# Input projection of the long-convolution block: seven products of half-size blocks in place of eight

## What is computed

```
def _centred_conv3(u, w, b):
    up = jnp.pad(u, ((0, 0), (1, 1), (0, 0)))
    return up[:, :-2] * w[0] + up[:, 1:-1] * w[1] + up[:, 2:] * w[2] + b

def _hyena_filters(L, ...):
    ...
    h = (a @ f_w3.astype(F32)).reshape(L, 2, HY_ORDER, D_MODEL)
    ...
    h = h * window[:, None, None, :]
    ...
    two_sided = two_sided / jnp.sum(jnp.abs(two_sided), 0, keepdims=True)
    return jnp.fft.rfft(two_sided, axis=0)

def _hyena(h, w_in, b_in, conv_w, conv_b, ...):
    u = _centred_conv3(h @ w_in + b_in, conv_w, conv_b)
    v, x1, x2 = jnp.split(u, 3, -1)
    ...
```

## Time and profile before

| | us |
|---|---|
| median of 3 runs | 3907.69 (3905.93 to 3911.46) |
| the profiled execution, its own time | 3907.51 |
| its span, first to last instruction | 3905.7 |
| PE busy in the span | 3610.5 (92%) |
| the stage's first matmul | at 58.87 |
| its last DVE copy to `u_staged` | from 496.05 to 496.74 |
| the next stage's first matmul | at 502.35 |

### The profile page before, as it was taken

The page is one execution under the profiler, slowest core; times in us unless marked ns, Lnnn a source line. Parts: engine busy times, 40 slices in busy tenths (PEclk is TensorE's granted clock), DMA queues, the critical chain, the costliest instruction groups (busy, mean ns, idle before and its releaser), DMA issues. The chain is left out here.

```text
span 3905.7 us, 63530 instructions
## 1 busy us (share of the span) xinstructions
PE 3610.5 (92%) x26142; PEld 2233.3 (57%) x26142; DVE 2554.0 (65%) x3451; ACT 884.7 (23%) x1758; POOL 461.4 (12%) x499
## 2 busy tenths in 40 slices
PE   6999989998879999999999998999976998868996
PEld 3444478884455555555555555544455898435563
DVE  5656379995876666767666674454076778557773
ACT  2000022221122221222212112322135443113232
POOL 0000000003100000000000001000031876001110
PEclk9999999998989999999999999999987999989998
DMA  7573322216589999999999995211002100228996
GB/s 278 218 261 138 143 76 109 117 76 239 219 285 361 335 328 327 326 335 329 328 328 333 332 325 205 89 56 70 33 1 90 37 4 4 100 92 315 357 357 226
DMA packets 289975, 798.58 MB, mean 204 GB/s; under 512 B 18728, under 2 KB 25904, under 8 KB 275120
## 3 DMA queue, kind: packets, MB, share of 16 engines
q1 hardware_dynamic: 271856, 719.02, 50.5%
q0 software_dynamic: 17136, 73.54, 5.9%
q10 hardware_dynamic: 720, 2.17, 0.2%
HBM read 708.56 MB, written 86.11 MB: 203 GB/s over the span
## 5 line engine op out<-in xcount | busy, mean ns | idle before, releaser
L1550 PE MATMUL banks<-moe_down,moe_hidT 128*128 128x512 f32 x1280 | 565.7, 595 | 9.4 <-DMA moe_down<-d_wd 9.3
L1550 PEld LDWEIGHTS banks<-moe_down,moe_hidT 128*128 128x128 f32 x1280 | 237.6, 191 | 281.5 <-issue 276.1
L1920 PE MATMUL banks<-hT,w_in_ring 128*128 128x512 f32 (+3 forms) x976 | 363.9, 535 | 1.9 <-ACT hT L1981 1.0
L518 PE MATMUL banks<-hT,w_in_ring 128*128 128x512 f32 x768 | 339.3, 596 | 1.4 <-PEq L212 1.4
L1623 ACT COPY moe_parts<-banks 128x512 f32<-128x512 f32 (+1 forms) x240 | 123.4, 514 | 840.7 <-PE banks L1529 837.7
L1529 PE MATMUL banks<-moe_wsums,moe_xsums 128*64 128x256 f32 x2560 | 301.3, 389 | 8.1 <-DVE moe_xsums L1667 4.0
L1920 PEld LDWEIGHTS banks<-hT,w_in_ring 128*128 128x128 f32 (+1 forms) x976 | 183.2, 188 | 180.7 <-issue 170.2
L1529 PEld LDWEIGHTS banks<-moe_wsums,moe_xsums 128*64 128x64 f32 x2560 | 181.1, 139 | 134.5 <-issue 49.1
L518 PEld LDWEIGHTS banks<-hT,w_in_ring 128*128 128x128 f32 x768 | 142.8, 190 | 185.2 <-issue 175.7
L757 PE MATMUL banks<-x_block,dft 128*128 128x256 f32 x896 | 196.5, 382 | 6.3 <-PEq L392 6.3
L757 PEld LDWEIGHTS banks<-x_block,dft 128*128 128x128 f32 x896 | 171.6, 192 | 30.3 <-issue 6.7
(11 more groups left out here) (479 smaller groups left out, 6015.8 us busy)
## 6 DMA issues: line engine op xcount, KB each, us to landing
moe_down<-d_wd SPq DMA_DIRECT2D x160, 1024.0 KB, 11.1
x_block<-d_wg SPq DMA_DIRECT2D x96, 1024.0 KB, 7.9
x_block<-d_wu SPq DMA_DIRECT2D x96, 1024.0 KB, 10.9
mix<-d_wg SPq DMA_DIRECT2D x64, 1024.0 KB, 8.8
mix<-d_wu SPq DMA_DIRECT2D x64, 1024.0 KB, 11.3
x_block<-d_seq SPq DMA_DIRECT2D x19, 1024.0 KB, 4.8
w_in_ring<-d_w_in SPq DMA_DIRECT2D x9, 2048.0 KB, 10.1
x_block<-d_mod_w SPq DMA_DIRECT2D x8, 2048.0 KB, 11.9
```

Source lines behind the costliest of these rows:

```text
L518: last = nc.tensor.matmul(m.ps[:, g % 2, :], ring[:, c, k, (mt % 4) * P:(mt % 4 + 1) * P], hT[:, k, h * BANK:(h + 1) * BANK], start=(k == ...
L1550: last = nc.tensor.matmul(m.ps[:, Y_BANK + h, :], hidT[:, j % 2, i * P:(i + 1) * P], wd[:, i, h * BANK:(h + 1) * BANK], start=(fc == 0 and ...
L1920: last = nc.tensor.matmul(m.ps[0:width, g % 6, 0:n], ring[:, q % 2, k, at:at + width], hT[:, k, first:first + n], start=(k == 0), stop=(k ...
```

## The change

Weights and tokens of the projection are cut into 2 by 2 blocks: two units make a pair (12 pairs, `n`), with `a11`, `a12` and `a21`, `a22` the lower and upper half of the channel sum for the first and second unit of the pair; `b11` to `b22` are the four quarters of `hT`. Each pair takes seven products P1 to P7 (Winograd's form of Strassen's scheme), each of 4 matmuls into one of banks 0, 1 and 5, in the order P1, P2, P6, P7, P5, P3, P4:

- The token sums `t1` to `t4` are made once, by DVE, as the stage starts (`t2` and `t4` lie in `x_block`, `t1` over `b12`).
- The weight sums are made by POOL, four sums of 128 by 512 in each pair, two of them in place in the ring.
- ACT writes only P1 (with the bias) to `u_padded`. DVE adds the other products from their banks (`added`), six times in a pair, and P7 in one sum of three operands: product, difference of the biases, and what was kept.
- `turn` is cut into single transposes of four tiles with one bank, 4, between them, spread over the next pair; `collect` likewise. `magnitudes` is cut in two.
- The window has one buffer: SP loads the next as soon as DVE has read the last. The matvec slots are halved (24 of 1 MB), since `t2` and `t4` take their room. In a pair SP loads slots 4n + 4 and 4n + 5, then stores `taps` of round n - 1 and loads the filter weights of round n + 1, then the window of round n + 1.
- At the end, `d_taps` of the next stage is loaded only after the last product.

```diff
@@ -180,8 +180,12 @@
...
-    sp.dma_start(m.window[:, b], m.dram["window"][j % NQ]).then_inc((m.ahead.win0, m.ahead.win1)[b], 16)
...
+def load_window(sp, m, j):
+
+    sp.dma_start(m.window[:], m.dram["window"][j % NQ]).then_inc(m.ahead.win, 16)
...
@@ -376,12 +381,11 @@
 
 def hyena_in_stage(nc, m):
...
+        nc.sbuf_tensor("token_diff", [P, KT // 2, BANK], F32) as t3,
+        nc.sbuf_tensor("w_diff", [P, KT // 2, P], F32) as s3,
...
         @block.sync
         def _(sp):
             def load_mv(n):
-                sp.dma_start(mv_ring[:, n % 2], mod_weights(m, GROUPS_IN[n // MV_SLOTS], n % MV_SLOTS)).then_inc(mv_in[n % 2], 16)
+                group, k = GROUPS_IN[n // KT], n % KT
+                name, at = ("mod_w", group) if group < MOD_GROUPS else ("ada_w", group - MOD_GROUPS)
+                sp.dma_start(mv_ring[:, n % 2], m.dram[name][:, k, at * MV_COLS:(at + 1) * MV_COLS]).then_inc(mv_in[n % 2], 16)
+
+            def next_mv(n, part):
+                for x in slots_of(n, part):
+                    if x + 2 < N_SLOTS:
+                        sp.wait_ge(s.mv_mm, x + 1)
+                        load_mv(x + 2)
...
+            for n in range(PAIRS_IN):
+                next_mv(n, 0)
+                next_mv(n, 1)
+                if 1 <= n <= N_IT:
+                    j = n - 1
                     sp.wait_ge(s.taps, j + 1)
                     sp.dma_start(m.dram["taps"][j], taps[:, j % 2]).then_inc(kept[j % 2], 16)
                     if j + 2 < N_IT:
                         load_filter(sp, m, j + 2)
-                if unit == 2 * N_IT + 1:
+                if n + 1 < N_IT:
+                    sp.wait_ge(s.gen_read, 8 * (n + 1))
+                    load_window(sp, m, n + 1)
...
+                kind, c = n // 4, n // 2 % 2
+                if n % 2 == 1 and kind + 1 < KINDS:
+                    sp.wait_ge(s.u_mm, 7 * (n + 1))
+                    load_input_chunk(sp, m, kind + 1, c)
...
             sp.dma_start(z, m.dram["seq"][2 * NQ]).then_inc(m.conv_ahead.z, 16)
+            sp.dma_start(x, m.dram["seq"][0]).then_inc(m.conv_ahead.x, 16)
+            sp.wait_ge(s.u_mm, 7 * PAIRS_IN)
             sp.dma_start(early_taps, m.dram["taps"][0]).then_inc(m.conv_ahead.taps0, 16)
-            sp.dma_start(x, m.dram["seq"][0]).then_inc(m.conv_ahead.x, 16)
...
+            def weight_sums(n):
+                kind, c = n // 4, n // 2 % 2
+                a11, a12, a21, a22 = (a_part(n, i, a) for i in range(2) for a in range(2))
+                if n % 2 == 0:
+                    pool.wait_ge(ready[c], (kind + 1) * 16)
+                if n:
+                    pool.wait_ge(s.u_mm, done(n - 1, P7))
+                nc.gpsimd.tensor_tensor(s3[:], a11, a21, ALU.subtract).then_inc(s.w_sums, 1)
+                pool.wait_ge(s.w_sums, 4 * n + 1)
+                nc.gpsimd.tensor_tensor(a21, a21, a22, ALU.add).then_inc(s.w_sums, 1)
+                pool.wait_ge(s.w_sums, 4 * n + 2)
+                pool.wait_ge(s.u_mm, done(n, P1))
+                nc.gpsimd.tensor_tensor(a11, a21, a11, ALU.subtract).then_inc(s.w_sums, 1)
+                pool.wait_ge(s.w_sums, 4 * n + 3)
+                pool.wait_ge(s.u_mm, done(n, P2))
+                nc.gpsimd.tensor_tensor(a12, a12, a11, ALU.subtract).then_inc(s.w_sums, 1)
+
+            def store(n):
+                pool.wait_ge(s.staged, 4 * (n + 1))
+                pool.dma_start(m.dram["seq"][n], stage[:, n % 2]).then_inc(stored[n % 2], 16)
+
...
+            def product(n, which, w, x):
+                for k in range(KH):
+                    last = nc.tensor.matmul(m.ps[:, bank_of(n, which), :], w[:, k, :], x[:, k, :], start=(k == 0), stop=(k == KH - 1))
+                last.then_inc(s.u_mm, 1)
+
+            for n in range(PAIRS_IN):
...
+                product(n, P1, a11, b11)
+                if n:
+                    pe.wait_ge(s.u_ready0, n)
+                product(n, P2, a12, b21)
+                if n < N_IT:
+                    filter_pair(4 * n)
+                for x in slots_of(n, 0):
+                    matvec_slot(x)
+                if n == 0:
+                    pe.wait_ge(s.token_sums, 2)
+                pe.wait_ge(s.w_sums, 4 * n + 3)
+                if n:
+                    pe.wait_ge(s.u_ready1, n)
+                product(n, P6, a11, t2)
+                if n < N_IT:
+                    filter_pair(4 * n + 1)
+                if n:
+                    turn(n - 1, 0, 0)
+                pe.wait_ge(s.first_kept, n + 1)
+                product(n, P7, s3, t3)
+                if n:
+                    turn(n - 1, 0, 1)
+                if n == 0:
+                    pe.wait_ge(s.token_sums, 4)
+                pe.wait_ge(s.c11, n + 1)
+                product(n, P5, a21, t1)
+                if n:
+                    turn(n - 1, 1, 0)
+                before = 4 * n - 1
+                if 0 <= before < N_SLOTS and before % KT == KT - 1:
+                    pe.wait_ge(s.taps, n - 1)
+                    matvec_columns(before // KT)
+                if 1 <= n <= N_IT:
+                    norms(n - 1)
+                if n < N_IT:
+                    filter_pair(4 * n + 2)
+                for x in slots_of(n, 1):
+                    matvec_slot(x)
+                pe.wait_ge(s.w_sums, 4 * n + 4)
+                pe.wait_ge(s.q, n + 1)
+                product(n, P3, a12, b22)
+                if n:
+                    turn(n - 1, 1, 1)
+                if n < N_IT:
+                    filter_pair(4 * n + 3)
+                pe.wait_ge(s.z_sum, n + 1)
+                product(n, P4, a22, t4)
...
+            for n in range(PAIRS_IN):
+                act.wait_ge(s.u_mm, done(n, P1))
+                if n:
+                    act.wait_ge(s.conv, 2 * n - 1)
+                nc.scalar.activation(u_part(0, 1), m.ps[:, bank_of(n, P1), :], ACT.Identity,
+                                     bias=m.cols[:, b_at + 2 * n:b_at + 2 * n + 1]).then_inc(s.first_kept, 1)
...
+            nc.vector.tensor_tensor(t3[:], b22, b12, ALU.subtract).then_inc(s.token_sums, 1)
...
+            v.wait_ge(s.token_sums, 1)
+            nc.vector.tensor_tensor(t2, t3[:], b11, ALU.add).then_inc(s.token_sums, 1)
+            v.wait_ge(s.token_sums, 2)
+            nc.vector.tensor_tensor(t1, b12, b11, ALU.subtract).then_inc(s.token_sums, 1)
+            nc.vector.tensor_tensor(t4, b21, t2, ALU.subtract).then_inc(s.token_sums, 1)
...
             def windowed(g):
                 j, r = g // 4, g % 4
                 if r == 0:
-                    v.wait_ge(win_in[j % 2], 16 * (j // 2 + 1))
+                    v.wait_ge(ahead.win, 16 * (j + 1))
...
-            gen = Steps(v, s.pair)
...
+            def added(n, product, out, kept):
+                v.wait_ge(s.u_mm, done(n, product))
+                return nc.vector.tensor_tensor(out, m.ps[:, bank_of(n, product), :], kept, ALU.add)
...
+            gen = Steps(v, s.pair)
...
+            for n in range(PAIRS_IN):
+                v.wait_ge(s.first_kept, n + 1)
+                if n:
+                    v.wait_ge(s.conv, 2 * n - 1)
+                added(n, P2, u_part(0, 0), u_part(0, 1)).then_inc(s.c11, 1)
+                if n < N_IT:
+                    windowed(4 * n)
+                if 1 <= n <= N_IT:
+                    larger(n - 1, gen)
+                v.wait_ge(s.c11, n + 1)
+                added(n, P6, u_part(0, 1), u_part(0, 1)).then_inc(s.q, 1)
+                if n < N_IT:
+                    windowed(4 * n + 1)
+                if n:
+                    collect(n - 1, 0, 0)
+                if 1 <= n <= N_IT:
+                    magnitudes(n - 1, gen)
+                if n:
+                    collect(n - 1, 0, 1)
+                if n == 0:
+                    v.wait_ge(s.bias_diff, 1)
+                v.wait_ge(s.q, n + 1)
+                v.wait_ge(s.u_mm, done(n, P7))
+                if n:
+                    v.wait_ge(s.conv, 2 * n)
+                nc.vector.scalar_tensor_tensor(u_part(1, 0), m.ps[:, bank_of(n, P7), :], bias_diff[:, n:n + 1], u_part(0, 1),
+                                               ALU.add, ALU.add).then_inc(s.z_sum, 1)
+                v.wait_ge(s.z_sum, n + 1)
+                added(n, P5, u_part(1, 1), u_part(1, 0)).then_inc(s.c22, 1)
+                added(n, P5, u_part(0, 1), u_part(0, 1)).then_inc(s.w, 1)
+                if n:
+                    collect(n - 1, 1, 0)
+                if n < N_IT:
+                    windowed(4 * n + 2)
+                if 1 <= n <= N_IT:
+                    direct(n - 1, gen)
+                if n == N_IT:
+                    scaled_taps(gen)
+                v.wait_ge(s.w, n + 1)
+                added(n, P3, u_part(0, 1), u_part(0, 1)).then_inc(s.u_ready0, 1)
+                if n:
+                    collect(n - 1, 1, 1)
+                if n < N_IT:
+                    windowed(4 * n + 3)
+                if n + 1 < N_IT:
+                    sum_diff(n + 1)
+                convolve(n, 0)
```

(25 more changed lines are left out.)

210 lines of the change are left out of this document (86 added, 124 removed).

## The result

The changed kernel takes **3918.6 us** (median of 8 runs, 3912.9 to 3922.0) where the kernel before takes 3908.3 beside it (3905.9 to 3915.7): ratio 1.0021, 95% interval 1.0012 to 1.0031. By the ratio it is slower by 8 us (5 to 12), not faster by the 5 that were forecast. Its profiled execution spans 3916.7 us. From there to the end both take nearly the same, 3409 and 3411. A stage is read from one profiled execution of each kernel, so a difference of a microsecond between two stages says nothing.

The account below looks back on a forecast made before the run. The prediction took TensorE (PE), busy 430.2 of 430.3 us, to bound the stage. Its terms, -41.2 + 24 + 6 + 1.5 + 1.5 + 3 = -5.2 us, gave 3902.5 us, range 3880 to 3916.

Parts of the forecast that it names:

- What the change removes (41.2): In the stage's products, 48 matmuls of two 0.429 us instructions each go, saving 41.2 us of PE.
- They land near T + 12.8: Filter weights land 12.8 us after T, the start of P3 in a pair; VectorE waits 6 us.
- The price of that wait (4.7 for 6 us; 24 in all): Late weights cost TensorE 4.7 us in each of four pairs and 5 in two more: 24 us back.
- A middle pair asks 36.2 us of PE: PE's work in one middle pair, products, filters, transposes, matvec slots and norms, takes 36.2 us.
- The start (6): In the first pair PE waits for VectorE's token sums, made ahead of the first filter's sums: 6 us.
- the clock (1.5): The wait at the start drops TensorE's clock once, costing 1.5 us.
- The other waits leave the clock alone: Waits of 1.8 and 2.5 us do not drop the clock, being shorter than the 2.6 it held.
- Collisions (1.5): GpSimd's weight sums and VectorE's sums in SBUF hold each other up; past the filters this costs 1.5 us.
- The tail (3): After the last product, copies and transposes alternate through one bank: 10.6 us in place of 7.6, 3 more.
- Late weights absorbed: Rival, chance 0.13: the filter weights' lateness is absorbed or absent, the 24 us stay saved; 3878 us.
- GpSimd and VectorE don't collide: Rival, chance 0.17: the chain is as forecast but the two engines' sums do not collide, saving 14 us; 3888 us.
- The clock falls at each wait: Rival, chance 0.10: each PE stop in the pairs drops the clock, ten falls of 1.9 us add 19; 3921 us.

Follow-up runs that it names:

- e5: The changed kernel with the edits of e1, e2 and e4 together; 3878.2 us, ratio 0.9921 to the kernel before.
- e6: e5 with the product P2 of each pair computed twice, the first time to no use; 3906.5 us, ratio 0.9995 to the kernel before.
- e11: e10 with GpSimd's two opening sums of a pair made ahead of its store; 3875.6 us, ratio 0.9917 to the kernel before.
- e12: e9 with GpSimd's two opening sums of the next pair made ahead of its store; 3921.7 us, ratio 1.0030 to the kernel before.
- e1: The changed kernel with each filter's weight rows asked for one pair earlier; 3888.7 us, ratio 0.9955 to the kernel before.
- e8: The changed kernel with the next filter's weights asked for just ahead of the 2 MB taps store; 3881.5 us, ratio 0.9926 to the kernel before.
- e2: The changed kernel with the first filter's weights summed ahead of the four token sums; 3910.9 us, ratio 1.0009 to the kernel before.
- e3: The changed kernel with three of GpSimd's four weight sums cut to a quarter of their columns (output wrong); 3914.5 us, ratio 1.0026 to the kernel before.
- e4: The changed kernel with the last pair's four transposes in four banks; 3913.6 us, ratio 1.0013 to the kernel before.
- e9: The changed kernel with GpSimd's 1 MB store held back until the next filter's weights are summed; 3929.2 us, ratio 1.0055 to the kernel before.
- e10: e8 with the edits of e2 and e4; 3877.8 us, ratio 0.9922 to the kernel before.

## Why the prediction was wrong

The mechanism was right: the filter weights land late behind the transfers that moved ahead of them, in the forecast pairs, and TensorE stops where it was said to. The size of that term was not right, and that decided the sign.

- **What the change removes (41.2).** Right as work: 672 instructions of L562 are there. As time some 30 to 35 of it can be had: 30 in e5 (by e6), since waits that the longer products hid appear, and 35 in e11.
- **"They land near T + 12.8"**: this is the step that failed. VectorE starts at T + 17.4 (190.09 less 172.69) and waits 10.7 us, not 6 (10.0 to 10.7 in the four pairs; 2.8 and 4.8 in the two behind them, where 3 was said). Of the 4.6 us missing, 2.3 are GpSimd's 1 MB store, issued at T + 5.4 and left out of the sum: without it the wait is 8.3 (e12). The rest is in small pieces: the second of the two loads is issued at about T + 1.6, not T + 0.8, takes 12.9 us without that store where 12 were reckoned, and VectorE starts some 0.6 after it lands.
- **The price of that wait (4.7 for 6 us; 24 in all).** 33 or 34 us by e1 and e8. Taking 40.5 us of wait away (e8) gave 34, 0.84 for one, where the forecast had 4.7 / 6 = 0.78. The range took the landing to be unsure by 1 us; it was off by 4.6. It also had TensorE waiting only for windowed sums at the next filter pair; behind so late a landing it waits 2.4 for the weights' sums first. And 1.1 of each 4.7 was for collisions with the late convolutions, which did not happen: all 16 steps of L740 and L742 in the four pairs take 1.28 or 1.29 us, not the 2.4 that were to be seen. One of 2.17 us comes in each of pairs 0, 5 and 6.
- **A middle pair asks 36.2 us of PE.** From one L664 to the next, e11 shows 37.3, 36.5 and 37.6 for the pairs that take 45.0, 43.7 and 44.6 in the changed kernel. Low by 0.9, but no part of the miss: the kernel before takes 40.0 or 40.9 us from one sum (L576) to the next, and less the removed 3.4 that is the same 36.5 or 37.4.
- **The start (6) and the clock (1.5).** 6.9 us of wait, and the work to P6 takes 2.4 us more at the lower level than in e2. Right in kind, short by 2; e2 gave 6.2 back. (3.3 us and four sums of 1.15 make 7.9, not the 7.5 that the prediction names.)
- **The other waits leave the clock alone.** So it was in the changed kernel: from 86 to 494 us it never left 1.00. But the reason given, that 1.8 and 2.5 are shorter than 2.6, does not hold: the clock fell behind waits of 2.12 and 2.30 (e2) and 2.31 (e3). That it held here was luck.
- **Collisions (1.5).** e3 took 4.8 off the stage. Half of it is the start, where the first filter pair began 14.0 us behind the first matmul (71.70 less 57.70) and in e3 11.6; the other 2.4 are the rest of the stage, near the 1.5, with two falls of the clock against them.
- **The tail (3).** 3.9, and e4 gave 4.3 back.
- **The rivals.** Late weights absorbed: no, 2 us are, 10.7 are not. GpSimd and VectorE don't collide: at the start they do, 3.27 for 2.29, in the four late pairs they do not. The clock falls at each wait: not in the changed kernel, whose 2.3 us waits leave it at 1.00; in e9 and e12 it fell nine and six times, and that is most of why their stages are longer. That its 3921 lies near the outcome is chance.

The sum can be closed by the chain of runs. The stage before, less 41.2, is 396.7 us; the weights add 34.2 (changed to e8), start and tail 10.3 (e8 to e10), the sums 1.1 (e10 to e11), and 6.2 are left in e11: together 448.5. The forecast had 24, 10.5 (with the clock), 1.5 and nothing for the last. So of the 16 us that it missed, 10 are the weights and 6 a remainder that it did not have. Of these 6 the trace of e11 shows 2.1 and 1.6 of waits (for the second windowed sums of pair 0 and for `u_staged`) and 1.7 of lower clock behind the first; about 1 is open. A split in another order would move a microsecond or two between the terms.

## What to carry to other kernels

When work is taken from the engine that bounds a stage, list every transfer that used to be early and add up all the bytes in flight ahead of it, those of the other queues too: here 0.25 MB of weights behind 5 MB made a loss of 8 us out of what is a gain of some 29 without it (e8, by the ratios). The cure was the order of two lines, and it was worth 34 us of stage. And ask of each new wait whether it is longer than the slack: in the pairs with matvec slots 2 us cost nothing, from there on each us cost most of one. When an experiment's time goes the wrong way, split the stage into TensorE's idle and busy time before blaming the waits: e9 idled no longer than the changed kernel, it worked at a lower clock.

## What the hardware showed that was not expected

- A GpSimd sum of 0.46 us lasted 2.38 beside a VectorE sum of 2.3 (e3), and VectorE's `bias_diff`, 0.16 us alone (e2), lasted 1.22 in the changed kernel beside a GpSimd sum. The Trainium skill (SBUF — State Buffer, "SBUF: two separate sides") calls the shared ports an exclusive lock held for the whole instruction; these rows agree, for a short operation pays the length of its neighbour. VectorE's sums that read the accumulator's banks (L717) had a mean of 0.69 us over 72, the 0.6 to 0.7 of before.
- GpSimd's store, issued 4.4 us after the weights, still delayed them by 2.4: what was issued later on another queue shared the 16 engines with what was waiting.
- The length of a wait did not decide whether the clock fell. A wait of 2.31 us in pair 3 left TensorE at 2.4 GHz in the changed kernel (granted clock 1.00 from 209 to 211 us); one of 2.31 in pair 2 of e3 was followed by 1.2 GHz (0.51 from 160 to 162 us), and so were waits of 2.12 in e2 and 3.36 in e12, while 2.36 was not in the changed kernel. A fall cost about 1.7 us. What else decides is open. The wait and the product behind it, first in the changed kernel, then in e3:

```profile
207.98 0.72 PE L521 MATMUL banks<-ident,u_conv 128*128 128x128 f32 x4 [2.31 <-DVE u_staged L658]
208.54 3.60 PE L562 MATMUL banks<-hT,w_in_ring 128*128 128x512 f32 x8
```

```profile
158.52 1.10 PE L521 MATMUL banks<-ident,u_conv 128*128 128x128 f32 x4 [2.31 <-DVE u_staged L658]
159.41 4.87 PE L562 MATMUL banks<-hT,w_in_ring 128*128 128x512 f32 x8
```
